# Order of bank reads, weight splits and buffer releases in the down projection of a two-layer encoder on one core

## The reference

```
h    = RMSNorm(x);  [q|k|v|u] = h @ w_in             # 2048 x 4096
attn = mixture of three dilated window attentions, 8 heads x 128
pool = centred means over 2/4/8/16 tokens, a 256x256 map per group
x    = x + RMSNorm(concat(RMSNorm(attn), RMSNorm(pool)) @ w_out)
f    = square(relu(RMSNorm(x) @ w_up)) @ w_down       # w_up 2048 x 8192, w_down 8192 x 2048
x    = x + RMSNorm(f)
```

## Time and profile before

| what | value |
|---|---|
| median of 3 runs | 1975.53 us |
| the profiled execution's own time | 1976.39 us |
| its span, first to last instruction | 1974.6 us |
| PE busy | 1915.5 us, 97% of the span |
| DVE busy | 1449.8 us, 73% |
| ACT busy | 982.6 us, 50% |
| mean granted TensorE clock | 0.985 |
| read from memory | 377.55 MB, 192 GB/s over the span |

### The profile page before, as it was taken

The page is one execution under the profiler, slowest core; times in us unless marked ns, Lnnn a source line. Parts: engine busy times, 40 slices in busy tenths (PEclk is TensorE's granted clock), DMA queues, the critical chain, the costliest instruction groups (busy, mean ns, idle before and its releaser), DMA issues.

```text
span 1974.6 us, 28391 instructions
## 1 busy us (share of the span) xinstructions
PE 1915.5 (97%) x10022; PEld 1696.2 (86%) x10022; DVE 1449.8 (73%) x1765; ACT 982.6 (50%) x1285; POOL 139.7 (7%) x178
## 2 busy tenths in 40 slices
PE   9999999989999998999999999999899899989988
PEld 7888888978988987898788888898799789879977
DVE  6985767875785687578778756778668847866886
ACT  6455656553444445345464556655444534444452
POOL 4910020000000000000200000200000000000002
PEclk9999999999999999999999999999999999999999
DMA  8664456575556556665576645565665666566663
GB/s 291 201 213 160 139 189 207 177 227 182 191 192 212 181 174 223 183 195 191 177 244 207 202 143 171 180 213 167 219 194 187 196 188 206 160 222 188 192 201 129
DMA packets 168326, 380.80 MB, mean 193 GB/s; under 512 B 11968, under 2 KB 14128, under 8 KB 167728
## 3 DMA queue, kind: packets, MB, share of 16 engines
q1 hardware_dynamic: 167904, 377.58, 59.2%
q10 hardware_dynamic: 336, 2.11, 0.3%
HBM read 377.55 MB, written 2.10 MB: 192 GB/s over the span
## 4 chain that ended last, share of the span: by engine, by line
PE 85%; DVE 6%; DMA 5%; issue 2%; ACT 2%; DVEq 0%; POOL 0%; SPq 0%; ACTq 0%; POOLq 0%
PE acc_pair L532 24%; PE acc_pair L537 12%; PE acc_pair L498 8%; PE acc_pair L499 8%; PE acc_pair L500 8%; PE acc_pair L831 6%; PE acc_pair L832 6%; PE acc_pair L833 6%; DMA raw<-in_w_down 4%; DVE w_lo L1329 4%; ACT w_hi L940 1%; PE o_bank L750 1%; DVE h_both L1383 1%; PE t_bank L831 1%; PE t_bank L832 1%
## 5 line engine op out<-in xcount | busy, mean ns | idle before, releaser
L1329 DVE TENSOR_TENSOR w_lo<-raw,w_hi 128x1024 fp32r<-128x1024 f32 x703 | 862.1, 1247 | 320.5 <-ACT w_hi L940 312.1
L940 ACT CAST w_hi<-raw 128x1024 fp32r<-128x1024 f32 x703 | 720.9, 1048 | 562.9 <-PE acc_pair L833 156.7
L532 PE MATMUL acc_pair<-h_both,w_hi 128*128 128x512 f32 x2176 | 560.2, 380 | 0.1
L532 PEld LDWEIGHTS acc_pair<-h_both,w_hi 128*128 128x128 f32 x2176 | 371.2, 191 | 30.2 <-ACT proj L1001 0.5
L537 PEld LDWEIGHTS acc_pair<-h_both,w_lo 128*128 128x128 f32 x2176 | 327.3, 191 | 29.1
L537 PE MATMUL acc_pair<-h_both,w_lo 128*128 128x256 f32 x2176 | 330.5, 274 | 0.0
L831 PE MATMUL acc_pair<-w_hi,f_hi 128*128 128x512 f32 x672 | 262.3, 390 | 34.3 <-DVE acc L1819 22.8
L832 PE MATMUL acc_pair<-w_lo,f_hi 128*128 128x512 f32 x672 | 261.0, 388 | 0.0
L833 PE MATMUL acc_pair<-w_hi,f_lo 128*128 128x512 f32 x672 | 260.2, 387 | 0.0
L831 PEld LDWEIGHTS acc_pair<-w_hi,f_hi 128*128 128x128 f32 x672 | 130.9, 195 | 55.9 <-DVE acc L1819 24.4
L498 PE MATMUL acc_pair<-w_hi,h_both 128*128 128x512 f32 x444 | 170.5, 384 | 1.4 <-DVE w_lo L1329 1.2
(11 more groups left out here) (242 smaller groups left out, 1867.2 us busy)
## 6 DMA issues: line engine op xcount, KB each, us to landing
raw<-in_w_up SPq DMA_DIRECT2D x256, 512.0 KB, 4.2
raw<-in_w_down SPq DMA_DIRECT2D x256, 512.0 KB, 4.7
raw<-in_w_in SPq DMA_DIRECT2D x128, 512.0 KB, 4.8
raw<-in_w_out SPq DMA_DIRECT2D x64, 512.0 KB, 5.3
x<-in_x SPq DMA_DIRECT2D x8, 256.0 KB, 7.6
w_pool_s<-in_w_pool SPq DMA_DIRECT2D x2, 1024.0 KB, 7.3
post_row<-in_g_mix_post SPq DMA_DIRECT2D x2, 1024.0 KB, 7.7
post_row<-in_g_ffn_post ACTq DMA_DIRECT2D x2, 1024.0 KB, 4.8
```

The costliest lines, as they stand in the source:

```text
L532: pe.matmul(acc_pair[b][:, m, :], w_hi[:, slot, col:col + P], x_both.rearrange("p s (a n) -> p s n a", a=2), start=(slot, k) == (0, 0), st ...
L940: act.copy(w_hi[:, half * PAIRS + p, :], raw[:, p, :]).then_inc(hi_made, 1)
L1329: dve.tensor_tensor(w_lo[:, slot, :], raw[:, p, :], w_hi[:, slot, :].bitcast(F32), ALU.subtract).then_inc(lo_made, 1)
```

## The change

Four edits, all in the feed-forward part.

1. On DVE, in the first double chunk of every group, the four sums of banks stand behind the first two blocks of the next chunk's weights and no longer behind the first six.
2. `t_used` is counted after each of the three products with `t_hi` and `t_lo`, and DVE waits for one third of them before each of its three writes to `t_sum`.
3. In the last group PE's unit c = 2 waits for the first bank of each token half only (`2 * CHUNKS - 3` in place of `- 2`); it writes no other.
4. In the last group ACT casts the first four blocks of unit c = 3 before it waits for `q_step`, and issues the gain row and takes the squares after them.

```
@@ seven, on PE
                     three(t_bank[1][:, :], sh[:, 0, :], sl[:, 0, :], t_hi[:, 0, :], t_lo[:, 0, :],
-                          p_first, p_last)
+                          p_first, p_last).then_inc(t_used, 1)
                     three(o_bank[:, :], sh[:, 1, :], sl[:, 1, :], t_hi[:, 1, :], t_lo[:, 1, :],
-                          p_first, p_last)
+                          p_first, p_last).then_inc(t_used, 1)
@@ group, on PE
-                        unit(hu + HU_GROUP - 4, r + 2 * CHUNKS - 2, f_hi, f_lo)
+                        unit(hu + HU_GROUP - 4, r + 2 * CHUNKS - 3, f_hi, f_lo)
@@ group, on ACT
-                    act.wait_ge(t_used, seven_no(l, g, len(SEVEN_AT)))
+                    act.wait_ge(t_used, 3 * seven_no(l, g, len(SEVEN_AT)))
                     for k, bank in ((0, t_bank[0]), (1, t_bank[1])):
                         act.copy(halves(q_sum[:, k, :]), put_back(bank[:, :])).then_inc(p_copied, 1)
+                    split_hi(hu + HU_GROUP - 2, 0)
                     act.wait_ge(q_step, 8 * (l + 1))
...
-                    split_hi(hu + 8 + c * 2 + 2, 0)
                     post_square(SQ_F, c * 2, r + c, 0, c)
@@ seven_lo, on DVE
-                    if not (isinstance(g, int) and l + g + n == 0):
-                        dve.wait_ge(t_used, no)
+                    again = not (isinstance(g, int) and l + g + n == 0)
+                    if again:
+                        dve.wait_ge(t_used, 3 * no - 2)
...
+                    if again:
+                        dve.wait_ge(t_used, 3 * no - 1)
                     dve.tensor_tensor(t_sum[:, 1, :], low_r, t_sum[:, 0, :], ALU.subtract
                                       ).then_inc(t_step, 1)
                     dve.wait_ge(t_step, 3 * no + 2)
+                    if again:
+                        dve.wait_ge(t_used, 3 * no)
@@ wide_pair, on DVE
                     if j == 0:
                         seven_lo(g, 2, hu + 2, 0)
                         seven_lo(g, 3, hu + 3, 1)
-                        split_lo(hu + 4, 0)
+                        split_lo(hu + PAIR_HALVES, 0, (0, 1))
+                        wide_sums(g, j, first)
+                        split_lo(hu + PAIR_HALVES, 0, (2, 3))
+                        split_lo(hu + PAIR_HALVES + 1, 1)
                     else:
                         for n in range(PAIR_HALVES - 1):
                             split_lo(hu + n + 2, n % 2)
-                    split_lo(hu + PAIR_HALVES + 1, 1, (0, 1))
-                    wide_sums(g, j, first)
-                    split_lo(hu + PAIR_HALVES + 1, 1, (2, 3))
+                        split_lo(hu + PAIR_HALVES + 1, 1, (0, 1))
+                        wide_sums(g, j, first)
+                        split_lo(hu + PAIR_HALVES + 1, 1, (2, 3))
```

## The result

| | before | changed kernel |
|---|---|---|
| median | 1977.28 us (4 runs, 1975.16 to 1979.59) | 1911.02 us (4 runs, 1910.78 to 1911.72) |
| profiled execution | 1976.39 us | 1911.72 us |
| its span | 1974.6 us | 1909.9 us |
| PE busy | 1915.5 us, 97% | 1892.6 us, 99% |
| mean granted clock | 0.985 | 0.999 |

The ratio to the kernel before is 0.9665, with a 95% interval of 0.9648 to 0.9682. The time went down by 66 us by the medians and by 64.7 us between the two profiled executions; forecast were 69.0 us and 1907 us, counted from the three runs with median 1975.53.

What follows compares the result with a forecast made beforehand. PE, busy 97% of the span, was taken as the bound, with DVE's order making it wait. 47.5 + 18.8 + 5.0 - 2.3 = 69.0 us less gave 1907 us, eight-in-ten range 1901 to 1919.

Steps and rivals of the forecast that it cites:

- Edit 1, waits: PE's eight waits for DVE's sums, one per group of each layer after the first double chunk, go: 47.5 us.
- the wait moves to block 2 or 3: Rival: PE waits instead for low parts of next blocks behind the sums, 2 us a place, 1923 us; chance 0.09.
- Edit 1, clock: Without the eight long waits PE's clock no longer falls to half, so slowed work after them speeds up: 18.8 us.
- the second rival: Half-clock stretches have their own beat, once per group, and stay, now wholly under work: 27.3 us back, 1934; chance 0.03.
- My reason that short waits cost no clock: PE's wait of 0.93 us brought no clock fall, so moved waits of 2 us were called too short for one.
- the rival of moved waits: PE waits for low parts of next blocks 2 or 3 behind the sums, 16 us in all, 1923; chance 0.09.
- Edit 2: At 24 handovers between pairs, DVE runs earlier and PE's small waits of 0.25 us go: 5.0 us gained.
- Edits 3 and 4: In each layer's last group, nothing from the bank wait; new PE waits from the later POOL products: 2.3 us lost.
- my replay: Layer 1's last group retimed with PE restarting earlier: waits of 0.8 us for a bank and 0.8 us for POOL.
- the last groups lose more: Rival: POOL costs 4 us a layer, plus a late next bank: 8 to 10 us lost, 1916; chance 0.08.
- rivals on order: Sums come late for another reason than the blocks before them, so only the pairs gain: 1970.5 us; chance 0.015.
- a starved ring: Weight buffers come back late, PE runs dry at blocks 4 to 8 at half clock: slower, 1980 us; chance 0.015.

Runs made afterwards that it cites:

- e7_behind0: The changed kernel with the sums of the first double chunk ahead of all blocks of the next chunk: 1936.95 us, ratio 0.9794.
- e6_behind4: The changed kernel with the sums of the first double chunk behind four blocks instead of two: 1920.97 us, ratio 0.9708.
- e4_no_thirds: The changed kernel with `t_used` again counted once a pair and waited for once: 1916.97 us, ratio 0.969.
- e10_pool: The changed kernel with POOL's products by the gain row in the last groups cut from 512 to 8 columns: 1906.24 us, ratio 0.9638.
- e8_behind3: The changed kernel with the sums of the first double chunk behind three blocks instead of two: 1913.94 us, ratio 0.9682.
- e12_spread: The changed kernel with combine moved earlier, one later sum delayed and the four sums spread out, all in the last groups: 1910.89 us, ratio 0.9661.

## Why the prediction held, point by point

**Edit 1, waits: right.** 47.5 us forecast. None of the eight waits is left, and the pauses between issues that vanished add up to 47.5 us. The first bank was complete before PE wanted it, blocks 2 and 3 came in time, and the rival "the wait moves to block 2 or 3" had no case in the middle groups. Even e7_behind0, which holds back all blocks, makes one wait and no second.

**Edit 1, clock: right.** 18.8 us forecast; the slower matmuls of the eight stretches cost 19.2 us, by the starts of the same matmuls in the two traces, and no stretch at 0.50 is left but the one at the end. That the stretches have their own beat (the second rival) is refuted: their number follows the long waits in every kernel run, eight before, none under work in the changed kernel, two in e6_behind4, four in e7_behind0. My reason that short waits cost no clock was too simple: it rested on one wait of 0.93 us, and the rival of moved waits, "2 us a place ... too short for the clock", rested on it too. The trace of before held a warning. I took one place, where the clock fell 4 us after PE's last issue; over the eight places it fell 2.4 to 5.5 us after it (at 1918.32 after a last issue at 1915.90), and e6_behind4 and e7_behind0 then showed the fall in pauses of 2.3 to 2.5 us.

**Edit 2: right.** 5.0 us forecast; the stretches with the pairs are 5.1 us shorter in the changed kernel, and undoing the edit costs 6.0 us by the medians, 4.8 at the pairs (e4_no_thirds). DVE's idle time before `t_sum` did not go to "near nothing": with its lead DVE now stands 0.5 us for the first product instead of 1.0 us for the last.

**Edits 3 and 4: the sign right, the size not.** I forecast 2.3 us of loss in the last groups; they lost 7.0. Both traces hold the same 10022 matmuls in the same order, so the starts can be compared one by one, and the difference of 64.7 us between the two profiled executions divides into 47.5 (pauses) + 19.2 (clock) + 5.1 (pairs) - 7.0 (last groups) - 0.2 (ahead of the first group). Two terms of my replay were too small.

The larger is POOL. I counted it in one wait of 0.8 us a layer. It makes four waits in each layer, 1.8 us of idle time in layer 1, and with the overlap and the stretched matmuls that each restart costs 2.8 us a layer between issues, 5.6 us in all. The smaller is the wait for the sum, 1.3 us more than before in both layers together where I had 0.7 (twice 0.8, less the 0.93 of before). In layer 1 I let the blocks of unit c = 2 end 10.7 us after PE's restart, with transfers of 4.7 us; the last one ended 11.8 us after it, at 1867.5. Its transfer was the second of four that SP issued 1.1 us apart, when the sums had let the buffers go in a bunch, and it took 6.1 us to land.

My rival "the last groups lose more" gave 8 to 10 us, and the loss of 7.0 us is nearer to it than to the forecast. Its time of 1916 was added up wrongly: 47.5 + 18.8 + 5.0 less 8 to 10 us gives 1912 to 1914. So the time of 1911 came out near 1907 because this term is small beside the 71.8 us of the other three, not because the last groups were understood.

**A reason that failed.** "By the rule the cost only moves with POOL's products, which speaks against edit 4" was wrong in its weight. Moved, the products cost PE about 5 us in both layers together (e10_pool); left where they were, they and the squares cost 23 us (18.4 more). The rule of the Trainium skill (SBUF — State Buffer, Who interferes with whom) agrees with all three traces in that the two slow each other, 2.2 us a low part beside POOL and 1.2 alone; whether one of them stands wholly, these times do not tell. What the rule does not say is which instructions have slack.

**The rivals on order and on a starved ring** are refuted: the first by e8_behind3 and e6_behind4, where blocks put back before the sums bring the waits back, the second by the changed kernel and by e7_behind0.

## What to carry to other kernels

When several edits remove a wait, price each one against the timeline that the others leave, since a sequence that costs nothing while its consumer is late can become the next bound (here 2 us alone, 18 us together). A bank of results should be read just after the work that the consumer needs first: two blocks too few cost 26 us of 1911, one and two too many cost 3 and 10 (one too few was not run). Look for the granted clock beside every pause of PE, for here two fifths as much again as the pauses came from it.

## What the runs showed of the hardware

Of 13 pauses between issues of 2.3 to 2.7 us (five with four blocks ahead, eight with none) six brought the granted clock from 1.00 to 0.50, each time for 3.4 us and wholly under work; the longest of the 13, 2.7 us, did not, and pauses of up to 2.1 us did not in any run. By the mean clocks of e6_behind4 the number of falls also differs from one execution of the same kernel to the next. Pauses of 4.6 to 10.3 us always did, for 3.4, 6.8 or 10.2 us. The Trainium skill (TensorE: Matmul & The Clock Gate, HAM oscillation — how this bites in real kernels) warns of idle gaps that are longer than these 13; these runs show the fall after shorter ones. A transfer of 512 KB took 3.8 to 4.9 us to land when the transfers were issued 2.2 us apart (before, 1938 to 1945); of four issued 1.1 us apart the first took 4.5 us and the others 6.1 to 6.4 (changed kernel, 1857.9 to 1861.3). It is not the distance alone: in e12_spread transfers 1.1 to 1.8 us apart took 4.2 to 5.5 us at one place (1855.1 to 1859.2).
